# Where TensorE sums the squares of four norms, who spreads the root, and in which order the next products open

## The reference, cut to what matters

```python
def rmsnorm(x, g):
    y = x * lax.rsqrt(jnp.mean(x * x, axis=-1, keepdims=True) + NORM_EPS)
    return y * g

x = x + merged @ w_out                        # first block
hn = rmsnorm(x, norm_ffn_g)                   # norm 3
x = x + (silu(hn @ w_gate) * (hn @ w_up)) @ w_down
x = rmsnorm(x, norm_final_g)                  # final norm, fused with the next one: norm 4
h = rmsnorm(x, norm_g[0]) * (1 + scale0) + shift0
x = x + 0.5 * gate0 * swiglu(h, ffn1_w1, ffn1_w3, ffn1_w2)
h = rmsnorm(x, norm_g[1]) * (1 + scale1) + shift1      # norm 5, then the mixer
x = x + gate1 * mixer(h)
h = rmsnorm(x, norm_g[2]) * (1 + scale2) + shift2      # norm 6, then the last FFN
```

## Time and profile before

| | us |
|---|---|
| median of 3 runs | 2006.15 |
| lowest, highest | 2005.57, 2012.10 |
| the profiled execution | 2008.66 |
| its span, first to last instruction | 2006.9 |
| mean granted TensorE clock | 0.991 |

### The profile page before, as it was taken

The page is one execution under the profiler, slowest core; times in us unless marked ns, Lnnn a source line. Parts: engine busy times, 40 slices in busy tenths (PEclk is TensorE's granted clock), DMA queues, the critical chain, the costliest instruction groups (busy, mean ns, idle before and its releaser), DMA issues.

```text
span 2006.9 us, 25390 instructions
## 1 busy us (share of the span) xinstructions
PE 1967.6 (98%) x9146; PEld 1585.0 (79%) x9154; DVE 1014.1 (51%) x1572; ACT 719.8 (36%) x1214; POOL 79.1 (4%) x117
## 2 busy tenths in 40 slices
PE   9998999999999999999999999999999999999999
PEld 7776777877888888888888878767777878888887
DVE  6756335656565554633334345767734653333322
ACT  5455434432222222332223234345534433222221
POOL 0001000001111000000000010400000000000000
PEclk9998999999999999899999999999999999999999
DMA  5211122327666554333332323211111223333332
GB/s 173 82 56 63 53 64 73 95 94 231 207 215 210 178 173 147 100 94 94 96 97 89 116 73 95 75 53 43 43 43 43 84 74 116 94 94 103 96 105 94
DMA packets 57521, 207.20 MB, mean 103 GB/s; under 512 B 6449, under 2 KB 6577, under 8 KB 57441
## 3 DMA queue, kind: packets, MB, share of 16 engines
q1 hardware_dynamic: 46800, 167.68, 27.0%
q0 software_dynamic: 10640, 38.44, 6.2%
HBM read 203.96 MB, written 2.10 MB: 103 GB/s over the span
## 4 chain that ended last, share of the span: by engine, by line
PE 89%; DVE 5%; ACT 3%; issue 2%; DMA 1%; SPq 0%; DVEq 0%; ACTq 0%; POOLq 0%
PE PS L437 26%; PE PS L439 25%; PE PS L438 25%; PE PS L862 2%; PE PS L897 2%; PE PS L881 1%; PE PS L667 1%; DMA ADA<-ada 1%; ACT HI L1046 1%; PE PS L559 1%; DVE BIAS L1808 0%; PE PS L590 0%; DMA X<-x_in 0%; PE PS L641 0%; DVE SM L1807 0%
## 5 line engine op out<-in xcount | busy, mean ns | idle before, releaser
L437 PE MATMUL PS<-XH,HI 128*128 128x512 f32 x1552 | 628.9, 405 | 9.8 <-DVE GATE_1M L1876 3.5
L1450 DVE TENSOR_TENSOR LO<-RAW,HI 128x1024 fp32r<-128x1024 f32 x311 | 382.9, 1232 | 456.1 <-ACT HI L1046 455.2
L439 PE MATMUL PS<-XH,LO 128*128 128x512 f32 x1552 | 607.9, 392 | 0.0
L438 PE MATMUL PS<-XL,HI 128*128 128x512 f32 x1552 | 607.2, 391 | 0.0
L1046 ACT ACTIVATE HI<-RAW 128x1024 fp32r<-128x1024 f32 x311 | 328.7, 1058 | 591.9 <-PE PS L439 586.3
L437 PEld LDWEIGHTS PS<-XH,HI 128*128 128x128 f32 x1552 | 293.4, 189 | 88.7 <-issue 26.5
L439 PEld LDWEIGHTS PS<-XH,LO 128*128 128x128 f32 x1552 | 292.7, 189 | 63.1
L438 PEld LDWEIGHTS PS<-XL,HI 128*128 128x128 f32 x1552 | 293.8, 189 | 53.1 <-issue 0.2
L437 PE MATMUL PS<-HIDH,HI 128*128 128x512 f32 x528 | 205.5, 389 | 0.0
L439 PE MATMUL PS<-HIDH,LO 128*128 128x512 f32 x528 | 205.5, 389 | 0.0
L438 PE MATMUL PS<-HIDL,HI 128*128 128x512 f32 x528 | 205.4, 389 | 0.0
(11 more groups left out here) (345 smaller groups left out, 2072.7 us busy)
## 6 DMA issues: line engine op xcount, KB each, us to landing
RAW<-weights SPq DMA_DIRECT2D x311, 512.0 KB, 3.6
ADA<-ada POOLq DMA_DIRECT2D x72, 512.0 KB, 4.6
X<-x_in SPq DMA_DIRECT2D x4, 512.0 KB, 7.1
y_out<-X SPq DMA_DIRECT2D x8, 256.0 KB, 4.6
SQC<-squares SPq DMA_DIRECT2D x1, 320.0 KB, 9.2
TAB_P<-positions POOLq DMA_DIRECT2D x1, 256.0 KB, 4.7
POS<-positions POOLq DMA_DIRECT2D x1, 256.0 KB, 3.3
LAMS<-lambdas POOLq DMA_DIRECT2D x1, 128.0 KB, 5.4
```

The source lines that it names most:

```text
L437: mm(bank, a, moving[0][:, t, :], start=start, stop=False)
L438: mm(bank, a, moving[1][:, t, :], start=False, stop=False)
L439: ins = mm(bank, z, moving[0][:, t, :], start=False, stop=stop)
L1450: V.tensor_tensor(LO[n0 % 3][:], RAW[n0 % 3][:], HI[n0 % 3][:].bitcast(F32), ALU.subtract)\
```

## The change

In norms 3 to 6, the square of tile 6 isn't added to RB[:, 0] any more. A new first_sums sums RB[:, 0] (tiles 0 to 5) and the square of tile 6 over partitions inside the last chunk's products; last_sums sums tile 7's square alone. In norm 4 the second set is treated alike, its last square is made on VectorE, and ada_sum(8) moves into behind. The table of the root is loaded before the last tile of x is waited for. VectorE spreads the first two of four root columns, ScalarE the other two. In behind, the four matmuls with a tile's high part come first, and the two with its low part wait for XL by themselves. The counts of keep_warm change.

```diff
-        WARM = [None, None, None, (1, 1, 2), (1, 1, 1), (1, 1, 2), (1, 1, 2)]
+        WARM = [None, None, None, (2, 1, 1), (2, 2, 1), (2, 1, 1), (2, 1, 1)]
+        G_LAST = SM2[:, 16:17]
-        SAB = ... n[0] - 1 ...
+        SAB = ... n[0] - (2 if k else 1) ...
             # TensorE
             def norm(k):
                 keep_warm(WARM[k][0])
-                norm_sums(k)
-                if k == 4:
-                    ada_sum(8, bank=4)
-                else:
-                    keep_warm(WARM[k][1])
+                last_sums(k)
+                keep_warm(WARM[k][1])
                 norm_spread(k)
...
+            def first_sums(k):
+                pe.wait_ge(sem("stds"), k)
+                if k == 5:
+                    pe.wait_ge(sem("finished"), DT)
+                pe.wait_ge(sem("sum_added"), SAB[k + 1])
+                pe.wait_ge(sem("squared"), NTB[k + 1] - 1)
+                for n, src in enumerate((RB[:, 0, :], SQ[:, 0, :])):
+                    for b in range(NB):
+                        mm(PS[:, 7, 8 + b:9 + b], src[:, b * P:(b + 1) * P], SQV["ones"][:, 0:1],
+                           start=n == 0 and b == 0, stop=False)
                 if k == 4:
+                    pe.wait_ge(sem("g_squared"), DT - 1)
+                    pe.wait_ge(sem("g_sum_added"), DT - 1)
+                    for src in (SUM_G, Y[:, 0, :]):
+                        for b in range(NB):
+                            mm(PS[:, 7, 12 + b:13 + b], src[:, b * P:(b + 1) * P], SQV["ones"][:, 0:1],
+                               start=False, stop=False)
+
+            def last_sums(k):
+                pe.wait_ge(sem("squared"), NTB[k + 1])
+                for b in range(NB):
+                    ins = mm(PS[:, 7, 8 + b:9 + b], SQ[:, 1, b * P:(b + 1) * P], SQV["ones"][:, 0:1], ...)
+                if k == 4:
+                    pe.wait_ge(sem("g_last"), 1)
+                    for b in range(NB):
+                        ins = mm(PS[:, 7, 12 + b:13 + b], Y[:, 1, b * P:(b + 1) * P], SQV["ones"][:, 0:1], ...)
                 ins.then_inc(sem("sq_summed"), 1)
             def norm_spread(k):
...
                 for b in range(NB):
+                    if k and b == NB // 2:
+                        pe.wait_ge(sem("expanded_second"), 2 * (k - 2))
             def behind(k, n0, banks):
                 for t in range(DT):
-                    pe.wait_ge(sem("split_lo"), SPLIT_TB[k] + t + 1)
+                    pe.wait_ge(sem("split_hi"), SPLIT_TB[k] + t + 1)
                     for g in range(2):
-                        ins = split_product(PS[:, banks[g], :], ws[g], (t,), (t,), (XH, XL), ...)
+                        mm(PS[:, banks[g], :], HI[ws[g]][:, blk], XH[:, t, :], start=t == 0, stop=False)
+                        mm(PS[:, banks[g], :], LO[ws[g]][:, blk], XH[:, t, :], start=False, stop=False)
+                    pe.wait_ge(sem("split_lo"), SPLIT_TB[k] + t + 1)
+                    for g in range(2):
+                        ins = mm(PS[:, banks[g], :], HI[ws[g]][:, blk], XL[:, t, :], start=False, stop=t == DT - 1)
...
+                    if k == 4 and t == 4:
+                        ada_sum(8, bank=4)
             # out_proj: in chunk m == 7, ahead of block 5;  ffn, f < 2: in chunk (i, j, g) == (3, 1, 1), ahead of block 4
+                    sums = {5: lambda: first_sums((3, 6)[b])} if m == DT - 1 else {}
+                                sums[4] = lambda: first_sums(4 + f)
             # ScalarE
+            def load_roots():
+                A(SM[:, 85:86], EPSC, ACT.Sqrt).then_inc(sem("table_loaded"), 1)
             def norm(k, first=0):
                 for t in range(first, nt):
                     square(k, t)
-                    if k == 4:
-                        square_g(t)
                 stds(k)
+                act.wait_ge(sem("rooted"), k - 2)
+                act.wait_ge(sem("rstd"), k)
+                for b in (2, 3):
+                    A(RB[:, 1, b * P:(b + 1) * P], SQV["ones"], ACT.Copy, scale=(FR if k == 4 else NR)[:, b:b + 1])\
+                        .then_inc(sem("expanded_second"), 1)
             # load_roots() is called ahead of the wait for the last x_added, in out_proj and in ffn with f < 2;
             # in ffn's last pair of tiles, square(6) and square_g(6) come behind the split of its first chunk, not its third
             # VectorE, roots_of(k)
+                if k >= 3:
+                    V.reciprocal(roots, NSTD).then_inc(sem("rooted"), 1)
+                    v.wait_ge(sem("rooted"), k - 2)
+                    v.wait_ge(sem("rstd"), k)
+                    V.tensor_copy(RB[:, 1, 0:2 * P]..., roots[:, 0:2]...).then_inc(sem("expanded"), 1)
+                    return
             # VectorE, the adding of tile 6's square
-                    if m:
+                    if 0 < m < DT - 1:
                         add_square(k, m - 1)
             # VectorE, ffn with f == 0, behind the last x_added
+                            V.scalar_tensor_tensor(out=Y[:, 1, :], in0=X[:, DT - 1, :], scalar=G_LAST,
+                                                   in1=X[:, DT - 1, :], op0=ALU.mult, op1=ALU.mult)\
+                                .then_inc(sem("g_last"), 1)
```

More of the change, by code:

```diff
@@ L232, in build @@
         NDB = np.cumsum([0, 1] + [n[0] for n in NORMS[1:]]).tolist()
-        SAB = np.cumsum([0] + [0 if k in (1, 2) else n[0] - 1 for k, n in enumerate(NORMS)]).tolist()
+        SAB = np.cumsum([0] + [0 if k in (1, 2) else n[0] - (2 if k else 1) for k, n in enumerate(NORMS)]).tolist()
         SPLIT_TB = np.cumsum([0] + [n[0] if n[4] is not None else 0 for n in NORMS]).tolist()
@@ L932, in out_proj @@
                         pe.wait_ge(sem("x_added"), XA[f"out{b + 1}"] + m - 3)
-                    used(split_product(PS[:, m % 4, :], w, range(8), range(8), (mh, ml)))
+                    sums = {5: lambda: first_sums((3, 6)[b])} if m == DT - 1 else {}
+                    used(split_product(PS[:, m % 4, :], w, range(8), range(8), (mh, ml), between=sums))
                 released["x_added"] += DT
@@ L973, in two @@
                                 pe.wait_ge(sem("hid_lo"), FT * f + 8 * g + blocks)
+                            sums = {}
+                            if f < 2 and isinstance(i, int) and (i, j, g) == (3, 1, 1):
+                                sums[4] = lambda: first_sums(4 + f)
                             used(split_product(PS[:, 2 + j, :], w, range(blocks), range(8 * g, 8 * g + blocks),
-                                               (HIDH, HIDL), first=g == 0, last=g == 2))
+                                               (HIDH, HIDL), first=g == 0, last=g == 2, between=sums))
                 two(0)
@@ L1384, in two @@
                             split_hi(n0 + 3 * j + g, 6, i)
[L1385 to L1389, removed]
+                            at_g = 0 if isinstance(i, int) and (i, j) == (3, 1) else 2
+                            if f < 2 and g == at_g and not (isinstance(i, int) and i == 0 and j == 0):
+                                act.wait_ge(sem("x_added"), 2 * i + (XA[f"down{f + 1}"] + j))
+                                square(4 + f, j - 1, i)
+                                if f == 0:
+                                    square_g(j - 1, i)
                 if f == 0:
@@ L1402, in ffn @@
                 if f < 2:
+                    load_roots()
                     act.wait_ge(sem("x_added"), XA[f"down{f + 1}"] + DT)
@@ L2032, in two @@
                                                    op0=ALU.mult, op1=ALU.add).then_inc(sem("x_added"), 1)
-                        if f < 2 and not (isinstance(i, int) and i == 0 and j == 0):
+                        if f == 0 and isinstance(i, int) and (i, j) == (3, 1):
+                            v.wait_ge(sem("x_added"), XA["down1"] + DT)
+                            v.wait_ge(sem("g_sum_added"), DT - 1)
+                            V.scalar_tensor_tensor(out=Y[:, 1, :], in0=X[:, DT - 1, :], scalar=G_LAST,
+                                                   in1=X[:, DT - 1, :], op0=ALU.mult, op1=ALU.mult)\
+                                .then_inc(sem("g_last"), 1)
+                        if f < 2 and not (isinstance(i, int) and (i, j) in ((0, 0), (3, 1))):
                             add_square(4 + f, j - 1, i)
```

33 lines of the change are left out of this document (17 added, 16 removed).

## The result

The kernel after takes 2014.79 us, median of 12 runs (2009.90 to 2017.88); the kernel before, in 12 runs on the same chip, 2009.43. The ratio is 1.0027 [1.0017, 1.0037]: 5.4 us slower, between 3.4 and 7.4. A second set of 12 gave 2012.87 and 1.0023 [1.0011, 1.0034]. Over all 24 runs the mean is 2013.9, over the 92 runs of the kernel before that came with the experiments 2009.1: 4.8 us slower. The forecast was 2007.5, with a range of 2003 to 2012.3: it missed the time. Its sign, a kernel slower by 1.3, was right.

The account below looks back on a forecast made before the run. TensorE, busy for 98% of the span, was taken to bound the kernel. Norm terms of +0.5 us and +0.8 for the clock made +1.3 on the base of 2006.15: 2007.5 us, range 2003 to 2012.3.

Parts of the forecast that it names:

- The base: Starting time the change was added to: 2006.15 us, median of three runs of the kernel before.
- The sums in the chunk: Last chunks before norms 3 to 6: early sums displace products, 1.8 us each, 3.5 in norm 4, 8.9 together.
- The rival of nearly free sums: Last chunks: one-column sums cost almost nothing, only the gaps' gains of 8.4 us remain, time 1997.8; chance 6%.
- The chain to Y: From E, the stage's last product issued, to Y, VectorE's first tile: 4.35 us, 5.9 in norm 4.
- Norm 5: Norm 5's chain: copy halved, no half clock, Y at E + 4.35; old E to N 20.2 against 20.59, -0.4 us.
- Where N is set: Third chunk's start N: VectorE's low part sets it, Y + 13.35, 14.05, 13.9; norm 4 Y + 14.8 by TensorE.
- Behind norm 3: TensorE's wait for the adaptation's first sum grows from 2.55 to about 2.9 us; norm 3 counts +0.9.
- The sum over the norms: Norms 3 to 6 together, old E to new N: +0.9, -0.5, -0.4, +0.5, in all +0.5 us without the clock.
- with the clock: Norm 4's last chunk: 32 sums in a row may bring half clock onto products, 1.7 us at even odds, +0.8.
- Norm 4 keeping its slow clock: Rival: norm 4's half clock of about 10 us stays, Y comes about 2 us later, time 2009.5; chance 15%.
- The clock falling behind 16 sums among products: Rival: clock falls in all four last chunks, 1.7 us each, 6.8 on +0.5, time 2013.5; chance 7%.

Follow-up runs that it names:

- g2: Kernel before plus one-column instructions without use in the last chunks, 16 each, 32 in norm 4; 2019.64 us, ratio 1.0054.
- f3: Kernel after with the root spread by VectorE alone, as before; one run, 2008.74 us.
- f4: Kernel before, unchanged, profiled a third time; 2012.58 us.
- g3: Kernel after, unchanged, run and profiled again; 2012.87 us, ratio 1.0023.
- f1: Kernel before, unchanged, profiled a second time; 2010.79 us.
- e1: Kernel after with the early sums moved from the last chunk into the gap, replacing keep_warm's first units; 2011.66 us, ratio 1.0014.
- f2: Kernel after with only RB (norm 4 also SUM_G) summed in the chunk, tile 6's square in the gap replacing keep_warm, memset later; 2010.85 us, ratio 1.0002.
- g1: Kernel after without sums in the chunk: VectorE adds tile 6's square early, RB summed right behind the chunk, memset later; 2004.25 us, ratio 0.9979.
- h1: Kernel after with all sums back in the gap and keep_warm counts of before, other parts kept; 2009.74 us, ratio 0.9998.
- e2: Kernel after with GpSimd's zeroing of QF and KF also waiting for norm 5's root; 2012.90 us, ratio 1.0018.

## Why the prediction was wrong, point by point

The mean of the 24 runs lies 6.4 us above the forecast: 2.9 are the base, 1.0 lies in the norms (the held copy of norm 5), and 2.5 lie outside them and stay open. The first set's median, from which the forecast is 7.3 off, is another 0.9 up.

**The base: 2.9 us, a term mis-sized.** I carried the change to 2006.15, the median of three runs. 92 runs of the same kernel have a mean of 2009.1. The profile showed 2008.66 and the highest run 2012.10; I noted the first and still moved down. With 2009.1 as the base the same terms give 2010.4.

**The sums in the chunk: right.** 16 instructions cost 1.8, 32 cost 3.5, with 1.7 for the half clock behind them where it comes, in four of six profiles. g2 puts 10.8 (7.6 to 13.9) on them against 9.7. The rival of nearly free sums is out: each instruction took 0.106 us in this stream too. The 25 ns that I took from the Trainium skill ("TensorE: Matmul & The Clock Gate", "Back-to-back issue gap") are its figure for the gap of a matmul taken alone; the same section says that in a stream of weight loads and matmuls the spacing is set by both, and here each has a load of 128 columns. The forecast took the table without that sentence.

**The chain to Y: right in three of four norms.** Forecast E + 4.35, and 5.9 in norm 4; it is 4.44 in norm 3, 4.49 in norm 6, 5.95 in norm 4. That the split spread gives nothing f3 shows.

**Norm 5: the step that failed.** Forecast E + 4.35, measured E + 5.42. "VectorE's copy is halved" took every copy for free to run. It isn't while GpSimd zeroes QF. The kernel before had the same hold, and its rows would have shown it: its copy there took 0.70 where the others take 0.43, to just behind the memset's end. Timeline of the kernel before, norm 5:

```profile
1185.21 3.50 POOL L382 MEMSET QF<- 2x4096 f32 x1 [350.12 <-DVE X L2030]
1187.61 2.00 PE L459 MATMUL PS<-SQC 128*128 128x512 f32 x2
1188.30 0.70 DVE L1513 COPY RB<-SM 128x512 f32<-128x512 f32 x1
1189.41 1.06 PE L514 MATMUL PS<-SQC,RB 128*128 128x128 f32 x4
```

1185.21 + 3.50 is 1188.71, and the copy ended at 1189.00. It cost nothing in this profile, since the transposes stood behind a unit of keep_warm at half clock until 1189.41. In f4, where norm 5 kept its clock, it did: the transposes waited 0.34 for the copy, and Y was at E + 5.55. So taking the half clock away, as the forecast did, could not bring Y to where the other norms have it. I never asked what GpSimd did. The change brought the copy 0.8 nearer to the memset's start, so that it gave that gain back.

**Where N is set: right.** The third chunk's first product waits for VectorE's low part in norms 3, 5 and 6 ([0.22 <-DVE LO], [0.41 <-DVE LO], [0.26 <-DVE LO]), at Y + 13.25, 13.95 and 13.80, forecast 13.35, 14.05 and 13.9; norm 4 is at Y + 14.86, forecast 14.8, TensorE's own. The 0.15 that the forecast put behind the low part for the semaphore stands in no row; in norm 3 it was 0.06 (446.21 to 446.27). Two of the rows, timeline of TensorE after:

```profile
446.27 0.50 PE L438 MATMUL PS<-XH,HI 128*128 128x512 f32 x1 [0.22 <-DVE LO L1491]
1209.06 0.50 PE L438 MATMUL PS<-XH,HI 128*128 128x512 f32 x1 [0.41 <-DVE LO L1491]
```

**Behind norm 3: a sign that failed.** The wait for the adaptation's first sum was to grow from 2.55 to about 2.9. It is 2.45 in the first profile after and 2.77 in g3, and 2.55, 1.39 and 2.62 in the three profiles of the kernel before: it scatters by more than the forecast change. What held is the term itself (+0.85 against +0.9).

**The sum over the norms.** Two profiles after and three before, means of the nets: norm 3 +0.85 (forecast +0.9), norm 4 +0.2 (-0.5, with the clock +0.3), norm 5 +1.1 (-0.4), norm 6 +0.1 (+0.5). Together +2.3 against +1.3. The difference is the held copy. The forecast was worked out from the first profile alone; against that one the nets are +0.75, +0.4, +0.75 and +0.7, 2.6 in all. Norm 6's +0.1 is small because f1 and f4 were 0.9 and 0.8 longer there, with their falls of the clock, and not because the change shortened it.

**What the runs say beyond that.** The runs differ by 4.8, so 2.5 lie outside what the norms show. The profiles have 1.7 of it in code that wasn't changed (means +3.4 after, +1.7 before), in stretches that scatter by as much from one execution to the next. More time at half clock is not the answer: over the runs the mean granted clock is higher after, 0.9922 against 0.9898. In the profiles norm 4's 10.2 us at half clock are gone, and so are the 3.4 in norms 3, 5 and 6 wherever before had them. This part stays open.

**The rivals.** Norm 4 keeping its slow clock (15%) did not happen in the kernel after. It happened in e1, f2, g1 and h1, which have less keep_warm ahead of the sums or between them. The clock falling behind 16 sums among products (7%) did not happen in norms 3, 5 and 6 of any profile; in the gaps it fell behind 24 and more (e1), and in profiles of the kernel before and of h1 behind 16. So the gain of the other parts in norm 4, 4.4 us of Y, was hardly one of moving ada_sum: as far as h1's one profile shows, it hung on the clock being kept. In the change that went with two units ahead of the last sums and half as many sums in the gap, and the early sums paid for both. Taken one by one: early sums +10.8 (g2), the eight instructions a norm less in the gap (16 in norm 4) 3 x 0.87 + 1.75 = -4.4, the other parts -0.4 (h1): +6.0, against 4.8 measured, where g2's and h1's shares are each uncertain by 3.

## What to carry to other kernels

Work moved from a gap into a full engine costs its whole length; first look for what can be done in the gap while something else is late, as g1 does with the first sums (with the later memset 4.2 us faster than before, 8.6 than the change). Products without use can be worth their time where the clock falls without them, but at half clock they block what stands behind them. Where a difference of 0.3% matters, take the base from dozens of runs, and look up in every engine's row, GpSimd's too, why one instruction of a kind is longer than its siblings.

## What the runs showed of the hardware

- A VectorE copy from SBUF to SBUF that is ready while GpSimd's memset runs ends only after it: 1.40 us against 0.29 (e2, same copy, memset moved), 0.70 against 0.43 in the kernel before. It ended 0.16 and 0.29 behind the memset's recorded end. The two-input operations on VectorE behind it kept their usual length while the second memset ran (two in 1.41). The Trainium skill ("SBUF — State Buffer", "Who interferes with whom") says that a copy can enter a mode in which it contends with GpSimd and that the second to issue is blocked until the first finishes; the trace agrees.
- The clock falls behind runs of one-column matmuls while TensorE is busy: in e1 in all four gaps, with no idle time between the products and the fall. It then stays down with TensorE busy: 10.18 of 10.20 us at 0.51 from 815.50 in the kernel before.
- A one-column float32 matmul that loads its own 128x128 weights takes 0.106 us for each of its two instructions at a granted clock of 1.00 (16 in 1.70 us) and 0.213 at half clock (16 from 816.98 to 820.39 in the kernel before).
- The same program spreads over 2000.6 to 2016.3 us in 92 runs, and 0.001 of mean granted clock goes with 1.56 us of it.
